# Two more weight loads ahead of the experts, and the experts' row work placed later

## The reference

```python
def _expert_choice_ffn(u, w_router, w_g, w_u, w_d):
    cap = CAPACITY_FACTOR * n // N_EXPERTS           # 2 * 512 / 16 = 64
    logits = jnp.einsum('bnd,de->ben', u, w_router)
    aff = jax.nn.softmax(logits, axis=1)
    gate, idx = lax.top_k(aff, cap)                  # each expert picks 64 tokens
    xe = u[bidx, idx]
    hg = jnp.einsum('becd,edf->becf', xe, w_g)
    hu = jnp.einsum('becd,edf->becf', xe, w_u)
    ye = jnp.einsum('becf,efd->becd', jax.nn.silu(hg) * hu, w_d) * gate[..., None]
    return jnp.zeros_like(u).at[bidx, idx].add(ye)
```

## Time and profile before

| | |
|---|---|
| median of 3 runs | 3060.25 us (3059.34 to 3063.01) |
| profiled execution | 3063.65 us, span 3061.6 us |
| TensorE busy | 2769.9 us, 90% of the span |
| VectorE, ScalarE busy | 1142.2 us, 783.0 us |
| loads of expert stages | layer 0 from 360.12 us, layer 1 from 1110.61 us |
| HBM read | 596.87 MB, 196 GB/s over the span |

### The profile page before, as it was taken

How to read it: one execution, slowest core, us unless ns; L and a number is a source line. 1 busy time by engine, 2 the same in 40 slices (tenths; PEclk the granted TensorE clock), 3 DMA queues, 4 the chain that set the end, 5 groups by cost and what they waited for, 6 DMA issues and landing times.

```text
span 3061.6 us, 31790 instructions
## 1 busy us (share of the span) xinstructions
PE 2769.9 (90%) x13316; PEld 1772.7 (58%) x13316; DVE 1142.2 (37%) x1674; ACT 783.0 (26%) x1218; POOL 124.7 (4%) x121
## 2 busy tenths in 40 slices
PE   6987789898879969989988999999999999999998
PEld 4534444343348644333335765878778756577886
DVE  4454522111253452111116534333333588332333
ACT  2343311010032131100004423322232465232122
POOL 1210200000000010000001000000000000000000
PEclk8998899999999979999998999999999899999999
DMA  8961279999942138999993212322232300122320
GB/s 293 323 236 37 119 299 427 428 412 428 427 192 83 70 138 361 427 428 420 428 426 138 82 56 83 110 83 97 83 115 59 83 1 1 41 104 83 110 90 35
DMA packets 125454, 601.01 MB, mean 196 GB/s; under 512 B 7248, under 2 KB 12688, under 8 KB 100480
## 3 DMA queue, kind: packets, MB, share of 16 engines
q1 hardware_dynamic: 120128, 584.27, 48.2%
q0 software_dynamic: 5184, 14.72, 1.5%
HBM read 596.87 MB, written 2.10 MB: 196 GB/s over the span
## 4 chain that ended last, share of the span: by engine, by line
PE 71%; DMA 14%; DVE 10%; ACT 4%; issue 1%; DVEq 0%; POOL 0%; SPq 0%; ACTq 0%; POOLq 0%
PE psum L285 69%; DMA weight_ring<-in_w_exp_down 7%; DVE scratch L235 4%; ACT scratch L273 4%; DMA scratch<-in_w_exp_down 3%; PE psum L300 3%; DMA weight_ring<-in_w_exp_up 2%; DVE scratch L3327 1%; DMA weight_ring<-in_w_exp_gate 1%; DVE scratch L268 1%; DMA weight_ring<-in_w_mix_in 1%; DVE scratch L1340 1%; DVE scratch L248 1%; DVE scratch L1701 0%; DVE scratch L731 0%
## 5 line engine op out<-in xcount | busy, mean ns | idle before, releaser
L285 PE MATMUL psum<-scratch,scratch 128*128 128x512 f32 (+13 forms) x8744 | 1792.3, 406 | 91.5 <-ACT scratch L273 24.9
L285 PEld LDWEIGHTS psum<-scratch,scratch 128*128 128x128 f32 (+4 forms) x8744 | 1320.8, 184 | 557.9 <-issue 212.9
L285 PE MATMUL psum<-weight_ring,scratch 128*64 128x512 f32 (+2 forms) x3104 | 777.1, 610 | 96.6 <-DMA weight_ring<-in_w_exp_down 40.3
L285 PEld LDWEIGHTS psum<-weight_ring,scratch 128*64 128x64 f32 (+2 forms) x3104 | 263.9, 144 | 553.4 <-issue 456.0
L273 ACT ACTIVATE scratch<-psum 128x512 f32<-128x512 f32 (+4 forms) x330 | 193.1, 585 | 1064.7 <-PE psum L300 572.5
L235 DVE TENSOR_TENSOR scratch<-weight_ring,scratch 128x2048 fp32r<-128x2048 f32 (+2 forms) x110 | 241.9, 2199 | 501.7 <-ACT scratch L273 500.3
L273 ACT ACTIVATE scratch<-weight_ring 128x2048 fp32r<-128x2048 f32 (+2 forms) x110 | 202.5, 1841 | 577.4 <-PE psum L285 554.9
L235 DVE TENSOR_TENSOR scratch<-scratch,psum 128x512 f32<-128x512 f32 x92 | 63.3, 688 | 522.6 <-PE psum L285 521.2
L235 DVE TENSOR_TENSOR scratch<-scratch,scratch 128x512 fp32r<-128x512 f32 (+12 forms) x358 | 210.5, 588 | 63.5 <-ACT scratch L273 51.1
L300 PE MATMUL psum<-consts,scratch 128*128 128x128 f32 (+1 forms) x1020 | 162.2, 300 | 64.9 <-DVE scratch L235 46.0
L273 ACT ACTIVATE scratch<-psum,scratch 128x128 f32<-128x128 f32 (+6 forms) x338 | 179.6, 531 | 153.1 <-PE psum L300 56.2
(11 more groups left out here) (103 smaller groups left out, 639.2 us busy)
## 6 DMA issues: line engine op xcount, KB each, us to landing
weight_ring<-in_w_exp_gate SPq DMA_DIRECT2D x50, 2048.0 KB, 15.7
weight_ring<-in_w_exp_up SPq DMA_DIRECT2D x44, 2048.0 KB, 15.8
weight_ring<-in_w_exp_down SPq DMA_DIRECT2D x44, 2048.0 KB, 14.2
weight_ring<-in_ffn_w SPq DMA_DIRECT2D x28, 2048.0 KB, 7.8
weight_ring<-in_w_mod SPq DMA_DIRECT2D x24, 2048.0 KB, 10.5
scratch<-in_w_exp_up SPq DMA_DIRECT2D x20, 2048.0 KB, 15.8
scratch<-in_w_exp_down SPq DMA_DIRECT2D x20, 2048.0 KB, 14.2
scratch<-in_w_exp_gate SPq DMA_DIRECT2D x14, 2048.0 KB, 15.8
```

The lines of the kernel that those rows point to most:

```text
L285: ins = T.eng.matmul(out, lhsT, rhs, start=start, stop=stop)
```

## The change

The ring gets two slots more at the head of each expert stage (`lend`), in the part of the memory of `xeT`, `high` and `low[0]` that isn't written yet. `xeT` and `high` are laid out by pairs of experts for that, so that pairs 0 and 1 lie ahead of the lent room, pairs 2 to 5 in one lent slot and pairs 6, 7 and `low[0]` in the other. SyncE waits in `lend` for the end of `MixerOut` on GpSimd also. The lent slots leave the ring at ("down", 0) and ("down", 1); the slot that lay over `low[1]` now leaves at ("down", 4), behind the loads of expert 5, not at ("up", 4). Rows, gates 0 and turned 1 now come behind up 1, rows 2 and 3 behind up 3 and up 5, gathers at experts 3, 4, 4, 5, 6, 6, 7, 7, and down always behind the gathers and the turning. The order of the loads is the same. `rows_out` waits for a later "y split".

```diff
+LENT_SLOTS = 2
...
+    def lend(self, Y, stage):
+
+        Y.wait_ge(*self.k.at("end", stage, "pool"))
+        self.slots += [len(self.base) + len(self.more) + i for i in range(len(self.lent))]
...
-    BESIDE = (1, 2, 3, 4, 5, 5, 6, 7)
+    BESIDE = (3, 4, 4, 5, 6, 6, 7, 7)
...
-        self.xeT = place(at, (NC, E * CAP))
-        self.high = place(at, (NC, E * CAP), F32R)
+
+        self.xeT = place(at, (E // 2, NC, P))
+        self.high = place(at, (E // 2, NC, P), F32R)
+        if not k.ring.lent:
+
+            k.ring.lent = [(place(at + 2 * NC * P + i * SLOT, [SLOT]), k.sem(f"lent_slot{i}_landed")) for i in range(LENT_SLOTS)]
...
             yield "up", e
-            if e == 0:
+            if e in (1, 3, 5):
+                yield "rows", (e + 1) // 2
+            if e == 1:
                 yield "gates", 0
-            if e in (0, 2, 4):
-                yield "rows", e // 2 + 1
-            if e % 2:
-                yield "down", e - 1
             yield from (("gather", c) for c in range(NC) if self.BESIDE[c] == e)
-            if e in (2, 4):
-                yield "turned", e // 2 + 1
-            if e and e % 2 == 0:
+            if e in (1, 3, 5):
+                yield "turned", (e + 1) // 2
+            if e:
                 yield "down", e - 1
             yield "flip", e
-            if e == 0:
-                yield "turned", 1
...
         k.ring.widen(Y, self.before)
+        k.ring.lend(Y, self.before)
         for what, e in self.order():
-            if (what, e) == ("up", 4):
-
-                k.ring.drop(len(k.ring.base) + MORE_SLOTS - 1)
+
+
+            given = {("down", 0): MORE_SLOTS + 1, ("down", 1): MORE_SLOTS, ("down", 4): MORE_SLOTS - 1}.get((what, e))
+            if given:
+                k.ring.drop(len(k.ring.base) + given)
...
         if p >= 2:
-            lane.wait_ge(*self.k.at(self.key, "y split", 2 * p - 4))
+            lane.wait_ge(*self.k.at(self.key, "y split", 2 * p - 3))
...
-            act(A, self.xeT[:, c, p * P:(p + 1) * P], k.psum.of(job)[:, c * P:(c + 1) * P], ACT.Identity,
+            act(A, self.xeT[:, p, c, :], k.psum.of(job)[:, c * P:(c + 1) * P], ACT.Identity,
...
-        ts(V, self.xeT[:, c, HALF:2 * HALF], k.psum.of(job), self.scale[:, c:c + 1],
+        ts(V, self.xeT[:, 4:8, c, :], k.psum.of(job).rearrange("p (a n) -> p a n", a=4), self.scale[:, c:c + 1],
...
-                x = self.xeT[:, c, e * CAP:(e + 1) * CAP]
+                x = self.xeT[:, e // 2, c, CAP * (e % 2):CAP * (e % 2 + 1)]
...
-            mm(T, bank, s, self.high[:, 4 * half:4 * half + 4, pair * P:(pair + 1) * P], pair == p0 and not last, False)
+            mm(T, bank, s, self.high[:, pair, 4 * half:4 * half + 4, :], pair == p0 and not last, False)
```

More of the change, by code:

```diff
@@ L144, in __init__ @@
     def __init__(self, k, base, more):
-        self.k, self.base, self.more = k, base, more
+        self.k, self.base, self.more, self.lent = k, base, more, []
         self.pieces = {}
@@ L154, in slot @@
     def slot(self, i):
-        return self.base[i] if i < len(self.base) else self.more[i - len(self.base)]
+        return (self.base + self.more + self.lent)[i]
     def widen(self, Y, stage):
@@ L1805, in turned_dve @@
             c = 4 + i
-            ts(V, self.xeT[:, c, p * P:(p + 1) * P], k.psum.of(job)[:, i * P:(i + 1) * P], self.scale[:, c:c + 1],
+            ts(V, self.xeT[:, p, c, :], k.psum.of(job)[:, i * P:(i + 1) * P], self.scale[:, c:c + 1],
                self.shift[:, c:c + 1], ALU.mult, ALU.add, *([("free", *job)] if i == 3 else []))
@@ L1934, in y_parts @@
         q, pair = slice(64 * (e % 2), 64 * (e % 2) + 64), e // 2
-        hi = self.high[q, :, pair * P:(pair + 1) * P]
+        hi = self.high[q, pair]
         lo, y = [x.rearrange("p (c n) -> p c n", c=NC) for x in (self.low_of(pair)[q, :], self.y[q, :])]
```

## The result

The changed kernel takes 3041.57 us (median of 4 runs, 3039.54 to 3044.53) against 3060.04 us before: the ratio is 0.9939, 95% interval 0.9921 to 0.9956. That is 18.5 us less by the two medians and 18.7 by the ratio, with an interval from 13.5 to 24.2. A second set of runs of the same kernel beside the experiments gave 0.9931 (0.9918 to 0.9944), 21.1 us less. Forecast were 3037.4 us and 22.9 us less. The direction and the path held, and the size was 2 to 4 us too large.

The account below looks back on a forecast made before the run. DMA transfers plus pauses, not TensorE, were taken to bound the expert stages. Pauses shrinking 12.2 us in layer 0 and 10.7 in layer 1, together 22.9, gave 3037.4 us from a median of 3060.25; own range 3034 to 3042, stated range 3032 to 3045.

Parts of the forecast that it names:

- The bound: Expert stages: the end is the start of transfers, plus the transfers, plus every microsecond in which the DMA stands still.
- The two lent slots: Head of each expert stage: pieces 5 and 6 go out with the first five, 9.8 us of transfer per layer.
- The first pause: DMA standstill before TensorE returns its first slot: 17.4 to 7.6 us in layer 0, 17.8 to 8.0 in layer 1.
- Pair 1's work behind up 1: Rows, gates and turning between up 1 and down 0: second pause stays 4.8 us, gain 0.0 and 0.1 us.
- the clock: TensorE's granted clock falls again behind gates 0, upon turning and down 0: 1.75 us, making the second pause 4.8, not 3.1.
- the second pause: DMA standstill before piece 14, near 440 us in layer 0: 4.8 us as before, 3.1 as the low end.
- The third pause: DMA standstill after TensorE's 4.16 us stop at the slots' transposes: goes, gaining 2.4 us in layer 0 and 0.8 in layer 1.
- The shares: Each DMA pause was sized as (1 - share) x width of a profile stretch, such as 0.87 x 20 = 17.4 us.
- Rival 3: Second pause grows: rows, gates or turning cost 5 us more, each layer gives back 5 us, 3047 us; chance 0.06.
- Rival 5: Slower: late y low part stops TensorE at rows of pairs 2 and 3 before turning and down; 3077 us, chance 0.04.
- The rate of the Trainium skill: Expert loads: HBM binding at about 358 GB/s, 5.9 us a piece, would close the first pause, 36 us, 3024.

Follow-up runs that it names:

- the run with the gates elsewhere: Changed kernel with gates of group 0 moved out of the stretch between up 1 and down 0: ratio 0.9950, or 0.9913 with PSUM banks turned back, against the kernel before.
- The order alone: Changed kernel without `lend`, so new order and layout but no lent slots: ratio 0.9982 against the kernel before, 5.5 us less.
- one lent slot: Changed kernel with one lent slot (over pairs 2 to 5) in place of two: ratio 0.9957 against the kernel before, 13.2 us less.
- the loads alone: Two lent slots with the job order of the kernel before, both leaving at ("down", 0): ratio 0.9985 against the kernel before, 4.6 us less.
- the run with the gates split: Changed kernel with gates 0 split: first pair behind turned 0, the others at expert 3; PSUM banks shifted: ratio 0.9950 against the kernel before, 15.3 us less.
- gather 7 first: Kernel before with one job exchanged, at expert 7 the gather ahead of down 6: ratio 0.9998 against the kernel before, 0.6 us difference.
- the split with the old banks: Changed kernel with gates 0 split and the PSUM bank ring turned on by seven at gates 1: 3032.23 us, ratio 0.9913 against the kernel before.
- the later start: Changed kernel with SyncE starting expert loads only after GpSimd's last split row: ratio 0.9924 against the kernel before; the change beside it 0.9931.

## Why the prediction was right, and where its sum was off

**The bound.** The length of a stage less its pauses is 467.6 us in layer 0 of the kernel before, and 467 to 471 us in both layers of every run here. So transfers plus pauses give the stage, to about 3 us.

**The two lent slots, 9.8 us.** The first pause shrank by 9.8 us in both layers, and TensorE's start was not touched. SyncE's wait for GpSimd cost nothing, and 7.7 us of lateness cost nothing either.

**Pair 1's work behind up 1, 0.0 and 0.1 us.** This term was mis-sized. The path was as I laid it out: piece 13 at 422.28 and piece 14 at 437.41 lie 29.5 and 44.6 us behind the first product, forecast 29.4 and 41.6 without the clock, 43.3 with it. The clock took more than the 1.75 us that I had from gates 1. There it had been at 0.50 for some 3.4 us; here it was so from 428.5 to 435.3 us, 6.8 us, and as long in both layers of the second profile. From the end of up 1 to the end of the last down 0 product TensorE needed 18.6 us in layer 0 for the 15.6 that the rows gave. In layer 1 it was 16.9 (1165.54 to 1182.42), with 3.4 us at the lower clock, and there the pause was 4.6. In the second profile it was 6.0 in both. So the second pause is 4.6 to 6.0 us, where I had 4.8, and costs 1.0 us more over both layers in the first profile and 2.4 in the second. The Trainium skill ("TensorE: Matmul & The Clock Gate", Part 4: PE-mode transpose) speaks of transposes that don't count as busy; here the turning ran at the lower clock (8 transposes in 1.95 us, 1.2 before) when it stood right behind the gates, and in the run with the gates elsewhere it took 1.21 us at 1.00 behind a wait. And in the changed kernel the clock fell at 428.5, inside the gates, 1.8 us before turning began. So the transposes did not bring the clock down; whether they kept it down longer stays open.

**What I read as a sum of two parts was an exchange.** The order alone closes the second pause, one lent slot leaves it almost closed, two open it again. I put the second pause at 4.8 us, "as long as before", with a gain of 0.0, and gave all of the 19.6 us at the head of the stages to the lent slots. The sum was right, the reading wasn't: the loads alone bring 5.5 us in the stages, the order alone 9.9, both 18.6 to 19.7, which is more than the two together. Until TensorE gives back piece 8's slot, 13 pieces can have gone out in the new order without lent slots, and 14 with one or with two, however early. With 14 the next one went out 83.27 us behind the first, so the pauses before that point together have a fixed length (13.6 us with two slots, 13.3 with one, layer 0). The second slot only moves it from one to the other, and what shortens it is work taken from TensorE in that stretch. The gates did that, for 10.7 to 11.8 us of the stages over both layers and, by the medians on one chip, 6.5 us of the time.

**The third pause, 2.4 and 0.8 us.** It went as forecast. By itself, in the kernel of before, that brought 3.6 us in the stages and nothing that the medians show.

**The shares.** My pauses came from DMA shares. By the bytes moved they are 0.5 to 0.6 us longer each, and the loads alone showed that a new pause costs this on top. For the change it matters little, since its number of restarts falls by one per layer. Between the 21.6 us that the pauses shrank (48.1 less 26.5 over both layers) and the 18.6 us of stage length in the first profile 3 us stay unplaced, more than the 1.3 us by which the 21.6 fall short of the 22.9 forecast; in the second profile the pauses shrank by 21.1 (48.1 less 27.0) and the stages by 19.7, and 1.4 us stay unplaced. So the mis-sized second pause accounts for a part of the miss only, and what made the rest stays open.

**From the stages to the whole.** The profiles wander elsewhere. The first expert stage begins at 353.8 to 360.1 us, and what lies behind the second takes 1454.6 to 1464.0 us, in the run with the gates split 1467.8; why the second part wanders isn't shown. The medians of the change, 18.7 and 21.1 us less, agree with the 18.6 and 19.7 us of its stages.

**Range and rivals.** 3041.57 lies in the forecast's own range of 3034 to 3042, near its upper end. Rival 3, a longer second pause, is what happened in part. Rival 5, a stop at rows 2 and 3, didn't show: from 450 to 600 us the share is 1.01. The rate of the Trainium skill ("DMA: Bandwidth & Descriptors", Where 436 GB/s comes from), about 358 GB/s, was not seen in a full stretch: it is 426 to 428 GB/s in every kernel here (480 to 610 us).

## What to carry to other kernels

When a stream of loads stands still, ask for each pause which engine's product gives the next slot back, and write the ledger through to the point where the stream no longer runs dry; more buffers ahead are worth little if the same number of pieces is allowed before the next hold-up. Then look for work in that stretch that can be done later or in an idle moment: it shortens the stage, while an idle stop elsewhere may be nearly free. Read the length of the stage in the profile beside the median. Where the stage is shorter and the kernel isn't, look behind the stage for a rotation of buffers that has shifted; in four runs here (the order alone, one lent slot, gather 7 first, the split with the old banks) the time gained 2 to 4 us less than the stages, with the change and the later start it gained as much or more, and only the time counts in the end.

## What was not expected of the hardware

The start of the transfers could be moved by 7.7 us with no effect. A pause costs about 0.6 us more in bytes than in DMA share (193 GB/s at a share of 0.51). The granted clock fell to 0.5 at gates 0 or behind them in both layers of the kernel before, for some 3.4 us, and of the changed kernel, for 6.8 us in three of four places, but not where most of the same products stood at expert 3; what makes the difference stays open. Kernels with the same work up to 350 us began the expert stage at 354 us, with a granted clock of 0.93 to 0.95 in that stretch, or at 358 to 360 us, with 0.90 or 0.91, and that wander is as large as a third of this change.
